# Order of the weight copies against exponentials and value reads in the attention stage of a hybrid decoder layer

## The reference

```python
s = einsum('bqkgd,bnkd->bkgqn', qc, k_cmp) - slopes * dist          # compressed keys
p_cmp = masked_softmax(s, dist >= 0);  o_cmp = p_cmp @ v_cmp
imp = einsum('bkgqn,nj->bkqj', p_cmp, ov)                            # scores of key blocks
_, idx = lax.top_k(where(forced, 1e4, where(valid, imp, -1.0)), 8)   # selected blocks
s = q . k_s[idx] - slopes * dist;  o_slc = masked_softmax(s, dist >= 0) @ v_s[idx]
s = q . k_w      - slopes * dist;  o_win = masked_softmax(s, 0 <= dist < 256) @ v_w
o = gate0 * o_cmp + gate1 * o_slc + gate2 * o_win
```

## Time and profile before

| | us |
|---|---|
| median of 3 runs | 1175.23 |
| lowest and highest run | 1174.79, 1177.73 |
| the profiled execution's own time | 1173.83 |
| its span, first to last instruction | 1172.1 |

### The profile page before, as it was taken

One profiled execution on the slowest core, in us unless ns is written; L12 is line 12 of the kernel. 1 busy time (PEld: TensorE's weight loads), 2 busy tenths in 40 slices (PEclk: granted clock), 3 DMA queues, 4 the chain that ended last, 5 costly groups with the idle time before them and its releaser, 6 DMA issues. The chain is left out here.

```text
span 1172.1 us, 14795 instructions
## 1 busy us (share of the span) xinstructions
PE 1100.9 (94%) x4873; PEld 663.2 (57%) x4874; DVE 684.3 (58%) x1543; ACT 306.6 (26%) x734; POOL 157.8 (13%) x193
## 2 busy tenths in 40 slices
PE   6999999999999999999999889999976999999995
PEld 3544574445566777777777778555543444444442
DVE  2422224344345666776666379643469788877883
ACT  3311121111333443343333455332211000000000
POOL 0020312200000000000000061000002233333332
PEclk9999999999999999999999899999987999999998
DMA  6310040120000000000000160521435988899432
GB/s 236 111 41 0 17 123 23 36 71 18 1 3 2 3 4 2 2 3 2 3 1 1 41 248 1 192 96 68 153 133 182 324 299 293 315 381 345 133 99 82
DMA packets 74177, 119.79 MB, mean 102 GB/s; under 512 B 14368, under 2 KB 53376, under 8 KB 74120
## 3 DMA queue, kind: packets, MB, share of 16 engines
q1 hardware_dynamic: 63032, 88.08, 22.2%
q0 software_dynamic: 11088, 30.95, 7.4%
HBM read 105.90 MB, written 21.50 MB: 109 GB/s over the span
## 5 line engine op out<-in xcount | busy, mean ns | idle before, releaser
L1567 DVE STREAM_TRANSPOSE big_w<-big_w 32x256 f32<-32x256 f32 x400 | 174.3, 436 | 16.5 <-DMA big_w<-hn_dram,misc 9.9
L1735 PE MATMUL ps<-ring_gate_up,big_w 128*128 (+1 forms) x400 | 182.0, 598 | 1.7 <-DVE big_w L1567 1.7
L511 PE MATMUL ps<-big_w,big_u 128*128 128x512 f32 (+1 forms) x448 | 174.9, 545 | 0.0
L1169 ACT ACTIVATE big_u<-ps,big_w 128x384 f32<-128x384 f32 (+15 forms) x192 | 90.2, 523 | 182.4 <-DVE big_w L1230 164.2
L1109 PE MATMUL ps<-ring_down,big_u 128*128 128x65 f32 x912 | 115.4, 275 | 16.8 <-DVE big_u L1245 8.6
L1109 PEld LDWEIGHTS ps<-ring_down,big_u 128*128 128x128 f32 x912 | 109.1, 192 | 36.7 <-ACT big_u L1178 15.1
L511 PEld LDWEIGHTS ps<-big_w,big_u 128*128 128x128 f32 x448 | 84.1, 192 | 76.3 <-issue 70.3
L1735 PEld LDWEIGHTS ps<-ring_gate_up,big_w 128*128 128x128 f32 x400 | 74.8, 192 | 87.3 <-issue 87.3
L1078 PE MATMUL ps<-ring_down,misc 97*128 97x512 f32 (+3 forms) x320 | 119.1, 481 | 1.3 <-ACT ring_gate_up L1188 1.3
L1991 PE MATMUL ps<-big_w,big_u 128*128 128x512 f32 x256 | 114.7, 595 | 0.9 <-ACT big_u L2133 0.9
L1230 DVE TENSOR_REDUCE big_w<-ps 128x2 f32<-128x768 f32 (+15 forms) x96 | 78.2, 814 | 58.7 <-PE ps L1083 49.8
(11 more groups left out here) (349 smaller groups left out, 1343.9 us busy)
## 6 DMA issues: line engine op xcount, KB each, us to landing
ring_gate_up<-in_w_gate SPq DMA_DIRECT2D x16, 1024.0 KB, 8.9
ring_gate_up<-in_w_up SPq DMA_DIRECT2D x16, 1024.0 KB, 11.5
ring_down<-in_w_down SPq DMA_DIRECT2D x16, 1024.0 KB, 13.5
misc<-in_x SPq DMA_DIRECT2D x16, 512.0 KB, 3.4
big_w<-in_w_in SPq DMA_DIRECT2D x6, 1024.0 KB, 8.4
big_w<-in_w_out SPq DMA_DIRECT2D x8, 512.0 KB, 7.5
hn_dram<-big_u SPq DMA_DIRECT2D x8, 512.0 KB, 2.7
out<-ring_gate_up SPq DMA_DIRECT2D x8, 512.0 KB, 3.6
```

What stands on the lines that cost most here:

```text
L511: last = nc.tensor.matmul(ps[:, b, 0:width], uT[:, k, c * P:(c + 1) * P], wbuf[:, n % 2, k, 0:width], start=(k == 0), stop=(k == KD - 1))
L1169: last = nc.scalar.activation(weights(j)[:, i * n:(i + 1) * n], src, ACT.Exp, bias=neg[:, br, h:h + 1])
L1567: last = nc.vector.transpose(dst[j * 32:(j + 1) * 32, :, i * 32:(i + 1) * 32], src[i * 32:(i + 1) * 32, :, j * 32:(j + 1) * 32])
L1735: last = nc.tensor.matmul(ps[:, 2 + b, :], xT[:, b, k, :], ring_gu[:, bass.ds(at + k * 2 * D_EXP, BANK)], start=(k == 0), stop=(k == KD - 1))
```

## The change

In the scalar stream `copy_weights(j-1)` is placed ahead of `exponentials(j)`. In the vector stream `copy_weights(j-1)`, the second bank, is placed ahead of `read_values`. Nothing is added, removed or resized.

```diff
@@ scalar stream
             for j in range(J + 1):
+                if j >= 1:
+                    copy_weights(j - 1)
                 if j < J:
                     exponentials(j)
-                if j >= 1:
-                    copy_weights(j - 1)
                 for c in z_copy_at.get(j, ()):
@@ vector stream
                 if j == 0:
                     gates()
+                if 1 <= j <= J:
+                    copy_weights(j - 1)
                 if j >= 2 and (j == J + 1 or slots[j - 2][0] != slots[j - 1][0]):
                     gi, br, u, heads = slots[j - 2]
                     read_values(gi)
@@
-                if 1 <= j <= J:
-                    copy_weights(j - 1)
                 if j in select_at:
                     select(*select_at[j])
```

## The result

The changed kernel takes 1163.85 us (median of 3 runs, 1161.28 to 1164.45) against 1175.23: ratio 0.989, 95% interval 0.987 to 0.991. The forecast was 1165.8, range 1160.5 to 1172.5. The profiled execution took 1163.85 us, with a span of 1162.1. Ratios and their intervals leave out an execution that is over 1.5% above the fastest of its kernel, which in this study is a single one, of 1183.28 us.

The account below looks back on a forecast made before the run. PE bounds the kernel, busy 1100.9 of 1172.1 us, so only its idle time could pay. Terms 5.1 + 1.1 + 2.1 + 0.7 + 0.9 + 0.25 - 0.8 gave 9.4 us, forecast 1165.8, range 1160.5 to 1172.5.

Parts of the forecast that it names:

- The last sign of being wrong: First SEL slot's maxima starting over 0.2 us later after the WIN slot's transposes than before would prove the prediction wrong.
- Item 1: Six rounds, 471.29 to 603.73, with both stalls at `values`: 5.1 us given back, bounds 0 and 10.2.
- Item 3: Vector stalls elsewhere: 2.1 us back at five places behind a read, and 0.7 of the 1.03 at 378.94.
- Item 4: Four weight-load waits for the scalar copy that PE's rows hide, as at 416.33: 0.9 us back.
- Items 2, 5 and 6: Round at 455.16: 1.1 us back; last selection's bank wait: 0.25 back; longer wait before first wide scores: 0.8 cost.
- At nothing: Later exponentials in every iteration, and reads now waiting behind a copy: both costed at zero, as covered by other work.
- The vector queue is not in the way: Rival: both stalls of the six rounds go; gain 14.5 us, 1160.7; chance of a larger gain 0.10.
- Only the vector part pays: Rival: scalar copy still late, ScalarE stalls stay; gain 2.8 us, 1172.4; chance 0.18.
- The slower case: Rival: `transposes(j)` waits for exponentials held past their 0.64 us slack; 3.5 us slower, 1178.7; chance 0.10.

Follow-up runs that it names:

- the kernel with the longer vector wait: Changed kernel with one 256-column vector addition of unused data ahead of the second WIN slot's copy in eight late units: 1170.98 us, ratio 0.993.

## Why the prediction was right, and by how much it was off

- *Direction, mechanism and size.* Forecast 9.4 us, measured 12.2 in the attention and 11.4 in the medians. The scalar waits went, the vector waits moved to the second WIN slot, the wait before the first wide scores grew from 1.33 to 2.00 (2.1 was forecast), and PE never waits for L1169.
- *The signs.* As said ahead: the scalar waits under 1 us (0.4, at the last selection), 7.5 us for L1245, two waits at the end unchanged, idle of ScalarE now behind L1178. Not as said: PE's busy time did change, by 3.6 us, and the six waits were 0.65 to 1.23 long, not 0.3 to 1.1. The last sign of being wrong, maxima of the first SEL slot over 0.2 us later after the transposes of the WIN slot, depends on which WIN slot is meant. Behind the second slot's transposes they start 1.46 us (590.30 less 588.84) instead of 0.85, so by the letter this sign came up; but that is PE being earlier, which the prediction's own numbers contain. Behind the first slot's they start 5.07 instead of 5.04, and that the queue gets no later is what the sign was for.
- *Item 1 was mis-sized by 1.9 us* (5.1 against 7.0). First, the vector queue is hardly later at all: the second copy starts at 591.31, and 602.07 less PE's lead of 10.79 at that round is 591.28, so 0.03 later and not 0.14. The copy started at 586.21, straight behind the maxima, 0.10 and not 0.15 behind the modelled end of the transposes, and the idle behind the read shrank from 0.21 to 0.15. At the two places of a round this gave 0.12 to 0.14 us more than the sum has, 0.8 in all. Second, the sum left out a stall behind each read of a WIN group, at `values` of the first SEL slot. In the timeline of before:

```profile
478.62 0.29 DVE L1245 COPY big_u<-ps 128x128 f32<-128x128 f32 x1
478.72 0.22 PE L1083 MATMUL ps<-masksb,identb 128*128 128x128 bf16 x1
...
479.06 1.30 PE L1109 MATMUL ps<-ring_down,big_u 128*128 128x65 f32 x10
```

  The copy ends at 478.91 and `values` starts 0.15 later, the lag of every wait for a vector copy here, but PE's row has no bracket, since the modelled end of the mask matmul (478.94) covers it. After:

```profile
472.12 0.29 DVE L1245 COPY big_u<-ps 128x128 f32<-128x128 f32 x1 [0.55 <-PE ps L1093]
...
472.94 0.22 PE L1083 MATMUL ps<-masksb,identb 128*128 128x128 bf16 x1
473.00 1.17 PE L1109 MATMUL ps<-ring_down,big_u 128*128 128x65 f32 x9
```

  Now the copy is long done, and `values` follows 0.06 behind the start of the mask matmul instead of 0.34. With the slot after it this gave 0.45 us in each of the first two rounds, 0.1 in the middle two and nothing in the last two, 1.1 in all.
- *Item 3 was mis-sized by about 1.0 us.* Behind 378.94 the transposes gained 1.2 where 0.7 was taken: there the queue didn't stand in the way. At the four places with rows of 0.36, 0.61, 0.36 and 0.39 us of idle they gained 0.51, 0.79, 0.51 and 0.39, as a row shows a wait short where a modelled end covers its start. Item 4 came out at about the 0.9 forecast. All in all the fall of PE's busy time by 3.6 us, with the same matmuls at the same clock, gives the size of what its rows had hidden, and the sum had 0.9 of it.
- *Items 2, 5 and 6* came out within 0.15 us.
- *"At nothing"*: the held exponentials cost nothing that shows, as holding them for 1.1 us more in 74 slots took 3.5 us in all and the early slots lost nothing. For the reads behind the copies PE's rows show no wait either.
- *The rivals.* "The vector queue is not in the way" is refuted for the six rounds: taking 1.25 us of queries out of it gave 7.2 us more. "Only the vector part pays" is the reverse of what the runs show: that part alone made the kernel 1.4% slower. The slower case had its place wrong. Held exponentials weren't a danger, but a wait of PE made longer was, by the clock that fell behind it, and the prediction had taken the clock of 1.00 as given for any order of the copies. That the three executions of the result show no such fall was in part luck: of nine later ones of the same kernel three took 1173.7 to 1174.9 us, outside the range that was forecast.

## What to carry to other kernels

When one engine's queue serves several consumers, put the copy that the bound engine waits for ahead of the work that has slack, and do it on all engines that feed the same consumer: with only one of two copies moved, the other one is waited for, and the next wait can grow by what was gained before it. After such a move look for the instruction that the next wait stands behind; moving a piece of preparation by one slot gave here another 7.2 us of attention, over half of what the change itself gave. And count the wait rows of a bound engine as a lower limit, since modelled ends can hide short waits in its busy time.

## What the runs showed of the hardware

PE's granted clock fell towards its lower level behind single waits of PE of 1.0 to 2.0 us in otherwise dense work, in the profiles shown for 4 to 10 us, which cost 3.3 us at one place and 4.4 at another. Most such waits had no fall behind them. In the attention of the twelve profiles, with the granted clock read in windows of 4 us, a fall followed 3 of 20 waits of 1.0 to 1.25 us, 9 of 19 of 1.3 to 1.7 and 1 of 6 of 2.0; one more fall, at 312 us, had no such wait before it. The kernel before has nine of these waits, of 1.03 to 1.33 us, and no fall in its profile. The same place differs between executions: the wait of 1.23 us in the changed order stands in three profiles at two places each, and one of the six had a fall behind it. In one execution 1.69 us passed and 1.68 didn't. So length isn't all that counts, and what else does is open. Behind the wait of 2.0 us for the last z copy it fell in the kernel with the longer vector wait, to 0.58, and in none of the other five profiles that have it:

```profile
372.00:378.00 6.00, 5.73 (x21) 4.14 (x22) 2.06 (x5) 0.42 (x2) 0.00 (x0) 0.58 0.01 3
```

Of the six executions with the queries earlier, where this wait is 2.0, two had a mean clock of 0.979 and less and took 1159.5 and 1166.0 us against 1153.3 to 1154.7 for the rest; the nine with the z copy first as well, where it is 1.3, all lie within 1152.0 to 1156.0 us. That fits, but nine and six are few, and it isn't shown that this wait is the cause. For a single-core kernel whose clock reads 1.00 in one profile, the order of two copies decided nevertheless over 20 us: the attention is 378.04 with the vector move alone and 351.72 with both, and about half of the 26.3 us between them, an estimated 13.6, is the clock (what the granted clock lacks of 1.00, times the length, over the windows of 4 us).
